# RWKV core of a hybrid decoder step: copies and products moved between the engines, a gate's scaling carried in factors, chain parts placed inside half rounds

## What is computed

```python
def _wkv_step(S, inp):
    r, k, v, w, kk, b = inp
    sa = jnp.einsum('bhij,bhj->bhi', S, -kk)
    S = S * w[:, :, None, :] + sa[..., None] * b[:, :, None, :] + v[..., None] * k[:, :, None, :]
    return S, jnp.einsum('bhij,bhj->bhi', S, r)

w_log = -jax.nn.softplus(-(w0 + jnp.tanh(mix(1) @ w1) @ w2)) - 0.5
decay = jnp.exp(-jnp.exp(w_log))
iclr = jax.nn.sigmoid(a0 + (mix(4) @ a1) @ a2)
kk = heads(k * k_k); kk = kk / jnp.maximum(jnp.linalg.norm(kk, axis=-1, keepdims=True), 1e-12)
k_h = heads(k * (1.0 + (iclr - 1.0) * k_a))
b_h = kk * heads(iclr)
S_T, o = lax.scan(_wkv_step, S0, xs)          # 512 tokens, 16 heads of 64
bonus = jnp.sum(r_h * k_h * r_k, axis=-1, keepdims=True) * v_h
```

## Time and profile before

| | us |
|---|---|
| median of 3 runs | 3632.11 |
| lowest, highest | 3629.02, 3633.79 |
| the profiled execution, time | 3627.32 |
| its span | 3625.5 |
| granted TensorE clock, mean | 0.983 |
| TensorE busy | 3442.5 (95%) |
| VectorE busy | 1941.2 (54%) |
| ScalarE busy | 1395.1 (38%) |
| GpSimd busy | 418.8 (12%) |

### The profile page before, as it was taken

How to read it: one execution, slowest core, us unless ns; L and a number is a source line. 1 busy time by engine, 2 the same in 40 slices (tenths; PEclk the granted TensorE clock), 3 DMA queues, 4 the chain that set the end, 5 groups by cost and what they waited for, 6 DMA issues and landing times.

```text
span 3625.5 us, 95343 instructions
## 1 busy us (share of the span) xinstructions
PE 3442.5 (95%) x40925; PEld 3228.3 (89%) x40925; DVE 1941.2 (54%) x3021; ACT 1395.1 (38%) x2344; POOL 418.8 (12%) x570
## 2 busy tenths in 40 slices
PE   7988899999999989999999999999899788999999
PEld 6977679999999855699999999999899666799999
DVE  7557755555346644365543446553374776465532
ACT  4535533443222533344432224442244454244421
POOL 0022221111000000011100101110000222211100
PEclk9999989999999999999999999999999999999999
DMA  3210002222222387422222222222222000122222
GB/s 121 93 38 5 4 26 93 81 85 85 87 87 80 121 305 297 171 84 81 81 90 88 88 82 84 81 86 88 88 76 88 10 4 27 40 85 86 81 90 85
DMA packets 97093, 314.74 MB, mean 87 GB/s; under 512 B 19074, under 2 KB 20354, under 8 KB 96018
## 3 DMA queue, kind: packets, MB, share of 16 engines
q1 hardware_dynamic: 88706, 288.79, 23.7%
q10 hardware_dynamic: 8080, 21.34, 1.6%
HBM read 297.30 MB, written 12.79 MB: 86 GB/s over the span
## 4 chain that ended last, share of the span: by engine, by line
PE 88%; DVE 7%; ACT 3%; issue 2%; DMA 0%; SPq 0%; DVEq 0%; ACTq 0%
PE ps L418 24%; PE ps L416 23%; PE ps L417 23%; PE ps L1462 4%; PE ps L1017 1%; PE ps L2045 1%; DVE m L1507 1%; PE ps L2144 1%; PE ps L1646 1%; PE ps L2080 1%; PE ps L1128 1%; PE ps L2100 1%; PE ps L1138 1%; DVE arb L1495 1%; PE ps L2052 1%
## 5 line engine op out<-in xcount | busy, mean ns | idle before, releaser
L416 PE MATMUL ps<-xh,wh 128*128 128x288 f32 x4656 | 1386.0, 298 | 3.0 <-DVE xl L2430 1.9
L418 PE MATMUL ps<-xh,wl 128*128 128x288 f32 x4656 | 1381.5, 297 | 0.0
L417 PE MATMUL ps<-xl,wh 128*128 128x288 f32 x4656 | 1358.7, 292 | 0.0
L391 ACT ACTIVATE wh<-raw 128x1024 fp32r<-128x1024 f32 x415 | 440.2, 1061 | 1247.5 <-PE ps L418 1209.4
L417 PEld LDWEIGHTS ps<-xl,wh 128*128 128x128 f32 x4656 | 888.9, 191 | 1.7 <-issue 0.5
L416 PEld LDWEIGHTS ps<-xh,wh 128*128 128x128 f32 x4656 | 876.1, 188 | 7.5 <-issue 3.5
L418 PEld LDWEIGHTS ps<-xh,wl 128*128 128x128 f32 x4656 | 873.6, 188 | 0.0
L398 DVE TENSOR_TENSOR wl<-raw,wh 128x1024 fp32r<-128x1024 f32 x415 | 508.4, 1225 | 519.7 <-ACT wh L391 513.8
L418 PE MATMUL ps<-hh,wl 128*128 128x288 f32 x1536 | 457.7, 298 | 0.0
L416 PE MATMUL ps<-hh,wh 128*128 128x288 f32 x1536 | 453.9, 295 | 0.0
L417 PE MATMUL ps<-hl,wh 128*128 128x288 f32 x1536 | 453.9, 295 | 0.0
(11 more groups left out here) (360 smaller groups left out, 4927.1 us busy)
## 6 DMA issues: line engine op xcount, KB each, us to landing
raw<-in_w SPq DMA_DIRECT2D x415, 512.0 KB, 3.5
kp<-in_cache_k SPq DMA_DIRECT2D x64, 512.0 KB, 5.5
vp<-in_cache_v SPq DMA_DIRECT2D x64, 512.0 KB, 5.8
rkv<-in_wkv ACTq DMA_DIRECT2D x2, 2048.0 KB, 9.7
out_wkvs<-rkv ACTq DMA_DIRECT2D x2, 2048.0 KB, 7.2
out_k<-qk ACTq DMA_DIRECT2D x1, 2304.0 KB, 8.2
out_v<-vg ACTq DMA_DIRECT2D x1, 2304.0 KB, 14.0
out_x<-x SPq DMA_DIRECT2D x8, 288.0 KB, 3.4
```

Source lines behind the costliest of these rows:

```text
L391: act.activation(wh[:, c % SPL], raw[:, c % RAWS], ACT.Copy).then_inc(s_hi, 1)
L416: pe.matmul(out, w_h, rhs_h, start=(first and k == 0), stop=False)
L417: pe.matmul(out, w_h, rhs_l, start=False, stop=False)
L418: mm = pe.matmul(out, w_l, rhs_h, start=False, stop=(last and k == nk - 1))
```

## The change

- d2 and d4 of the prompt's inverse become "move": VectorE copies them (one 128 x 256 copy). "cross" (d2t, d4t) goes to ScalarE, two half-height copies. Counts of a_e and a_d, and GpSimd's wait for d2t, follow.
- L1182 goes to ScalarE as an Identity with scale and bias 0.5, in piece 4 behind the second tanh; the scan waits for it.
- L1189 is dropped. zz1 stays a tanh, so t3 and kh carry a factor of 2 and b a factor of 2, pinv is taken with a bias of ln 0.5, and the bonus gets a factor 0.5.
- b's product moves from GpSimd to VectorE, (zz1 + 1) x kraw, in piece 10 behind the bonus product.
- In a stop TensorE's products are cut in two halves (2 chunks each): even place, first half, odd place, second half. On ScalarE, VectorE and GpSimd the whole of `inv_step` comes behind the odd place.

```diff
@@ -5,6 +5,8 @@
+import math
@@ -141,6 +143,7 @@
         qg8, gneps, eps, warm, root5 = small[:, 0:1], small[:, 1:2], small[:, 2:3], small[:, 3:4], small[:, 8:13]
+        halves, lnhalf = small[:, 4:5], small[:, 5:6]
         big = m.at
@@ -1178,17 +1181,13 @@
             if k == 4:
-                dve.wait_ge(a_zz, B.cnt(2, 1))
-                dve.tensor_scalar(zz0, zz0, 0.5, 0.5, ALU.mult, ALU.add).then_inc(a_sg, 1)
                 after(dve, a_ex, B.cnt(3, 0))
-                dve.wait_ge(a_sg, B.cnt(2, 1))
+                dve.wait_ge(a_sg, B.cnt(1, 1))
                 dve.tensor_tensor_scan(flat(csum[:, 0]), mview("scan", 0 if B.prompt else 1), flat(zz0), 0.0,
...
                 dve.wait_ge(a_zz, B.cnt(2, 2))
-                dve.tensor_scalar(zz1, zz1, 0.5, 0.5, ALU.mult, ALU.add).then_inc(a_sg, 1)
                 dve.wait_ge(a_cm, B.cnt(1, 1))
-                dve.wait_ge(a_sg, B.cnt(2, 2))
                 if B.prompt:
@@ -1209,7 +1208,7 @@
                 dve.wait_ge(a_kh, B.cnt(2, 1))
-                dve.scalar_tensor_tensor(kh[:, 0], t3, 1.0, row, ALU.add, ALU.mult).then_inc(a_kh, 1)
+                dve.scalar_tensor_tensor(kh[:, 0], t3, 2.0, row, ALU.add, ALU.mult).then_inc(a_kh, 1)
             if k == 10:
@@ -1220,9 +1219,11 @@
                     dve.tensor_tensor(t3, t3, B.per(PC["rk", j]), ALU.mult).then_inc(a_rk, 1)
+                dve.wait_ge(a_kk, B.cnt(1, 1))
+                dve.scalar_tensor_tensor(bb, zz1, 1.0, kraw[:, 0], ALU.add, ALU.mult).then_inc(a_bb, 1)
             if k == 13:
                 dve.wait_ge(a_bo, B.cnt(1, 1))
-                dve.tensor_tensor(B.row(rkv, KD), z, B.row(rkv, 2 * KD), ALU.mult).then_inc(a_bon, 1)
+                dve.scalar_tensor_tensor(B.row(rkv, KD), z, 0.5, B.row(rkv, 2 * KD), ALU.mult, ALU.mult).then_inc(a_bon, 1)
                 after(dve, a_co, B.tile(NCK, -2 * NCK))
@@ -1281,10 +1282,12 @@
                 half_tanh(act, B, zz1, KD).then_inc(a_zz, 1)
+                act.wait_ge(a_zz, B.cnt(2, 1))
+                act.activation(zz0, zz0, ACT.Identity, scale=0.5, bias=halves).then_inc(a_sg, 1)
             if k == 8:
...
                 act.wait_ge(a_cs, B.cnt(1, 1))
-                act.activation(pinv[:, 0], csum[:, 0], ACT.Exp, scale=DECAY).then_inc(a_ex, 1)
+                act.activation(pinv[:, 0], csum[:, 0], ACT.Exp, scale=DECAY, bias=lnhalf).then_inc(a_ex, 1)
                 act.wait_ge(a_cm, B.cnt(1, 1))
@@ -1303,9 +1306,6 @@
                 pool.tensor_tensor(pprev[:, 0], csum[:, 0], zz0, ALU.subtract).then_inc(a_cm, 1)
-            if k == 10:
-                after(pool, a_kk, B.cnt(1, 1))
-                pool.tensor_tensor(bb, kraw[:, 0], zz1, ALU.mult).then_inc(a_bb, 1)
             if k == 12:
@@ -1317,9 +1317,9 @@
             ktok=("kst", "ist", 0, "copy", "", "ktok", ()),
-            d2=("m2", "m1", 0, "copy", "", "m3", ("lt", "ktok")),
+            d2=("m2", "m1", 0, "move", "", "m3", ("lt", "ktok")),
             d2t=("m1", "m2", 2, "cross", "", "m4", ("et",)),
-            d4=("m4", "m3", 2, "copy", "", "m1", ("d2", "d2t")),
+            d4=("m4", "m3", 2, "move", "", "m1", ("d2", "d2t")),
             d4t=("m3", "m4", 0, "cross", "", "m2", ()),
@@ -1370,14 +1370,14 @@
             return [(name, part) for r in rounds_of(prompt) for part in range(2) for name in r
-                    if steps_of(prompt)[name][3] == "copy"]
+                    if steps_of(prompt)[name][3] in ("copy", "cross")]
...
                 for part in range(2):
-                    out += [(name, part) for name in r if steps_of(prompt)[name][3] != "copy"]
+                    out += [(name, part) for name in r if steps_of(prompt)[name][3] not in ("copy", "cross")]
                     if "lt" in r and prompt:
@@ -1433,9 +1433,9 @@
-        def inv_pe(pe, B, k, part):
+        def inv_pe(pe, B, k, part, behind):
             inv, names = steps_of(B.prompt), rounds_of(B.prompt)[k]
-            for name in names:
+            for name in names if not behind else ():
                 if name == "lt":
@@ -1453,7 +1453,7 @@
                         after(pe, a_d, B.own("d", others_of(B.prompt).index((need, part)) + 1))
-            for p in range(4 * part, 4 * part + 4):
+            for p in range(4 * part + 2 * behind, 4 * part + 2 * behind + 2):
                 for name in names:
@@ -1464,23 +1464,32 @@
                     mm = l_pe(pe, Bat(B.j, B.c + 1), p)
-            mm.then_inc(a_m, 1)
+            if behind:
+                mm.then_inc(a_m, 1)
...
-        def inv_act(act, B, k, part):
+        def inv_act(act, B, k, part, behind):
+            if not behind:
+                return
             sl, inv, of = slots[B.s], steps_of(B.prompt), slice(4 * part, 4 * part + 4)
...
                 _, _, bk, how, _, to, _ = inv[name]
-                if how == "copy":
-                    if name == "d4":
-                        act.wait_ge(a_p1, B.own("p", 1))
-                    act.wait_ge(a_m, B.own("m", 2 * k + part + 1))
-                    act.activation(sl[to][:, of], half_of(bk, part), ACT.Copy).then_inc(a_e, 1)
...
-        def inv_dve(dve, B, k, part):
+                if how not in ("copy", "cross"):
+                    continue
+                act.wait_ge(a_m, B.own("m", 2 * k + part + 1))
+                if how == "cross":
+                    for r, cross in zip(HEADS, HEADS[::-1]):
+                        op = act.activation(sl[to][r, of], half_of(bk, part)[cross], ACT.Copy)
+                else:
+                    op = act.activation(sl[to][:, of], half_of(bk, part), ACT.Copy)
+                op.then_inc(a_e, 1)
...
+        def inv_dve(dve, B, k, part, behind):
+            if not behind:
+                return
             sl, inv, names = slots[B.s], steps_of(B.prompt), rounds_of(B.prompt)[k]
@@ -1499,13 +1508,13 @@
                 _, _, bk, how, by, to, _ = inv[name]
-                if how == "copy":
+                if how in ("copy", "cross"):
                     continue
+                if name == "d4":
+                    dve.wait_ge(a_p1, B.own("p", 1))
                 dve.wait_ge(a_m, B.own("m", 2 * k + part + 1))
-                if how == "cross":
-                    for r, cross in zip(HEADS, HEADS[::-1]):
-                        op = dve.tensor_copy(sl[to][r, of], half_of(bk, part)[cross])
-                    op.then_inc(a_d, 1)
+                if how == "move":
+                    dve.tensor_copy(sl[to][:, of], half_of(bk, part)).then_inc(a_d, 1)
                 elif how == "add":
@@ -1517,14 +1526,16 @@
-        def inv_pool(pool, B, k, part):
+        def inv_pool(pool, B, k, part, behind):
+            if not behind:
+                return
             sl = slots[B.s]
...
             if k == 1 and part == 1 and B.prompt:
-                after(pool, a_d, B.own("d", others_of(True).index(("d2t", 1)) + 1))
+                after(pool, a_e, B.own("e", copies_of(True).index(("d2t", 1)) + 1))
                 pool.tensor_tensor(plus[:], sl["m4"][:], mview("ist").unsqueeze(1).to_broadcast([P, NCK, CT]),
@@ -1599,11 +1610,10 @@
                     for behind in range(2):
-                        if behind:
-                            inv_step(eng, inv, k, part)
                         for q, pos in enumerate(CHAIN_AT if chain else ()):
...
                                 chain_part(eng, chain, q // 3, q % 3)
+                        inv_step(eng, inv, k, part, behind)
                     for piece, pos in enumerate(PREP_AT if prep else LAST_AT):
@@ -2535,6 +2545,8 @@
             dve.memset(gneps[:], GN_EPS)
+            dve.memset(halves, 0.5)
+            dve.memset(lnhalf, math.log(0.5))
             dve.memset(eps[:], RMS_EPS)
...
```

## The result

The changed kernel takes 3656.9 us (median of four executions, 3650.4 to 3667.8) against 3631.5 us, a ratio of 1.0073 [1.0047, 1.0099]. It is slower by 25 us, outside the range of 3612 to 3645. So the two traces lie 40 us apart, the medians 25; lengths read from this trace are rather too long. Of the executions behind the experiments three are far off (one of the kernel before 9044 us, one of e7 3956, one of e8 4779); the ratios and the slope further down leave them out.

What follows compares the result with a forecast made beforehand. No engine is full, so only TensorE's waits at its 22 stops count. Twelve full halves -1.2, two first -0.7, two preparing +0.4, two of the sample group -0.6: -2 us of 3625.5; median taken as 3630, range 3612 to 3645.

Steps and rivals of the forecast that it cites:

- rivals A and C: A: same time, waits at stops 4, 14 and L1138 go but return at stop 7, chance 0.43; C: see rival C.
- the two halves that prepare the sample group: Tanh in eight pieces, scan 2 us later, but two products freed of the standstill: +0.4 us for both.
- Part 1, the scan's path: Stops 2 to 7: scan 1.0 us later behind ScalarE's copies and Identity; loss 0.7 us, between 0.2 and 1.3.
- The shift at stop 8: TensorE reaches stop 8 at about 355.85 instead of 355.2 us: 0.7 later, between 0.2 and 1.3.
- rival C: Slower: ScalarE's queue shifts stop 8 beyond the 0.9 us that later waits can swallow; at 1.5, 3642 us; chance 0.23.
- Part 2, b's product: Stops 9 to 13: without GpSimd's product VectorE doesn't stand still, both products take 1.36 against 1.57 us; gain 0.36, twice.
- Part 3, the split: Chain parts inside half rounds: 0.33 + 0.24 = 0.6 us gained at places 29-30, up to 0.3 lost at even-to-odd places.
- The gain of 0.6 us around place 30: Places 29-30: eviction goes first (0.66 in place of 0.99 us), and the part lies half a stop earlier (0.24).
- from there to the end VectorE's adds and masks set the pace, and those don't change: From stop 16, reached at -0.1 us, to the half's end: VectorE's unchanged work sets the pace.
- its sign, a wait of over 1.5 us at stops 6 and 7: Rival C's mark: TensorE's wait around stops 6 and 7 over 1.5 us.

Runs made afterwards that it cites:

- e7: Changed kernel with d2, d4 back on ScalarE and d2t, d4t on VectorE, zz0's scaling staying on ScalarE: 3631.73 us, 0.9995.
- e8: e3 with one wait more, GpSimd's addition of the identity to m1 waiting for r's factor on VectorE: 3619.93 us, 0.9960.
- e6: Changed kernel with zz0's scaling back on VectorE, d2t and d4t staying on ScalarE: 3635.86 us, 1.0010.
- e14: Changed kernel with whole rounds in stops 0 to 8 and the split in stops 9 to 21: 3642.96 us, 1.0028.
- e5: Changed kernel with unread filler products on TensorE, 4 and 6 pairs before two waits of the chain: 3646.35 us, 1.0033.
- e4: Changed kernel without the split (whole rounds, order inside a stop as before); copies, scaling and b's product as changed: 3639.66 us, 1.0027.
- e11: Changed kernel with the Identity moved ahead of the second tanh on ScalarE: 3660.05 us, 1.0080.
- e3: Kernel before with b's product on VectorE behind the bonus product, iclr's gate factor carried and L1189 dropped: 3619.77 us, 0.9965.
- e2: Changed kernel with copies and zz0's scaling taken back; b's product on VectorE, factors and split kept: 3625.58 us, 0.9982.
- e15: e3 with the split only in stops 9 to 15: 3619.94 us, 0.9961.
- e9: e4 with zz0's scaling back on VectorE, so moved copies and b's product in whole rounds: 3626.93 us, 0.9989.

## Why the prediction was wrong

**The missing step: TensorE's clock.** The sum took every wait of TensorE as so many microseconds, one for one. Nowhere does it ask what a wider gap does to the granted clock, though the earlier trace rows has the column, and shows 0.97 for the cores and 1.00 for the half. In the sum this is a term put at nothing. The runs price it in three ways. Within e6: 2.7 us a half between halves with and without the fall, with the state no later. Between the changed kernel and e14, at the same lateness of the state: 1.9 us by the spread, 2.1 over the half. Between the changed kernel and e5: 10.5 to 24 us. A fourth, weaker one is the spread of the executions themselves: over the 83 executions of the kernel before that went with the experiments, time falls by 1.7 us for each 0.001 of mean clock; the changed kernel has 0.974 against 0.981, 12 us by that slope. Ten full halves at 2.1 to 2.7 us make 21 to 27 of the 33 us that the cores lost in the profiled execution, the slowest of the four; over the medians, 25 us apart, it is 10.5 to 24 (e5), and nearer to the 12 of the slope if the other executions, with their higher clock, fell less often. In e5, where the clock is held, 3646.4 less up to 13.7 for the filler is 3633 or more: at a held clock the change would be between no difference and 13 us of loss. That is where rivals A and C stood. A second term was far off too: the two halves that prepare the sample group, put at +0.4 us, took some 7.5 more in the profiled execution. Their clock fell further as well; how much of it is the clock's was not tested.

**Part 1, the scan's path.** The walk through ScalarE's queue was right in order and in size: half-height copies 0.77 us a pair (0.8 taken), Identity 0.71 (0.62 taken), scan 1.1 us later (1.0 taken). The shift at stop 8 was put at 0.7, at most 1.3. With the clock held in most or all full halves it is 0.8 (e14), 1.1 (e5, filler included) and 1.2 us (e4), so inside the bounds but in their upper half, and in two of the three above the 0.9 from which the prediction let rival C decide. With the clock's fall it is 2.7. The term was sized for the scan; e11 shows that what counts is the state: 1.4 us late in the changed kernel (8.86 to 10.29). The prediction named sst behind the Identity, and put its lateness into the same 0.7.

**Part 2, b's product.** The mechanism is right, the size probably too small. The bonus product takes 0.75 us wherever GpSimd has no product beside it, 1.57 where it has. The Trainium skill (SBUF — State Buffer, "SBUF: two separate sides") says that a VectorE operation with two SBUF inputs and a GpSimd operation that reads SBUF exclude each other; e3 and e8 agree, with 1.57 to 0.75 and 0.97 to 0.69 us. I counted 0.36 us for each first half and 0.2 for a full one, some 3 us. By e3 it is 1.3 and 0.45, some 7 us, and 12.7 between the medians. The two profiled executions lie 5.8 us apart, so the traces have nothing more to place. e3's mean clock is 0.983 against 0.982 in the kernel before, so a part of it may be the clock's.

**Part 3, the split.** The gain of 0.6 us around place 30 is there: from the bonus sum to sst 5 3.99 us before, 3.40 after; 4.07 in e4, 4.03 in e3, 3.40 in e2. The step that failed is "from there to the end VectorE's adds and masks set the pace, and those don't change": I let the 0.6 stand in the sum all the same. If VectorE sets the pace there, chain parts that come earlier wait longer; that it is VectorE was not tested. From sst 5 to the end it is 6.69 us before and 7.33 after, 6.55 in e3 and 7.18 in e15, which has whole rounds there again. And what the split costs in the early stops, where it stands between ScalarE's copies and the chain's evictions, was not in the sum: with the queue it is 17 us (e4 to the changed kernel), nearly all by way of the clock, for where the clock is held the split kernel's half is as long as e4's (31.83): 32.3 in e5, of which up to 0.7 are the filler. With the scaling back on VectorE it is 8 to 9 (e9 to e6), and the four fallen halves of e6 make up the difference between the full halves (4 x 2.7 us against 10 x 1.04).

**The rivals.** C named the right place and the right engine. Its condition, over 0.9 us at stop 8, held in e5 and e4 and just not in e14; its sign, a wait of over 1.5 us at stops 6 and 7, is 1.37 us in the half shown and at most 1.8. It gave 3642, about what the kernel takes with the clock held in most halves (e14 3643, e4 3640), but the 14 us beyond that go with falls of the clock, which C doesn't have either. It was given 0.23 because the average of ScalarE, 16.2 of 32 us, left room; the table of 2 us windows would have shown in the kernel before that TensorE's thinnest stretch (busy 1.28 of 2.00 us, at 352 to 354) is just where the change adds waiting. That was to be had before the run. Whether the clock would then fall was not: e4 and e14 are thinner there and mostly keep it.

**What stays open.** Why the split brings the clock down where e4 and e14, with TensorE as thin, mostly keep it. Why e2 lies 6 us above e3 although its full halves are shorter. How the 25 us divide exactly between waiting and clock, since a filler that holds the clock costs time itself; a version with the same waits and the clock held for nothing was not found.

## What to carry to other kernels

When a change lets TensorE wait longer in a stretch where it is already thin, read its busy time and its granted clock there in windows of a few microseconds, and put the fall of the clock down as a term of its own, with a chance, since the busy time alone did not tell here whether it falls: where it fell it cost 2 to 2.7 us a half, on top of 1.4 us of lateness. Of work moved to an engine with room on average, count what then stands in front of the evictions that a serial chain on TensorE waits for, and not only the step that was moved. A gain in the middle of the half is no gain of the half until the rest has been followed to its end.

## What the runs showed of the hardware

The granted clock of TensorE fell inside a kernel whose TensorE is 95% busy, once in each of ten full halves, in the half shown after a stretch of 2 us in which it was busy 0.63 us, with no single wait above 1.4. From 326 to 332 us it stood at 1.2 GHz, while TensorE had no idle time at all. The same code did it in some halves and not in others, with the same busy time ahead (e6), and 0.53 busy in 2 us left it at 2.4 GHz in most halves of e4 and e14.

A half-height copy on ScalarE, 64 x 256, took 0.38 us, as long as the full-height one of 128 x 256, and a pair 0.77: a cross copy in two pieces costs twice the whole one. The Identity over 128 x 512 with scale and a bias column took 0.71 us; the Exp with the bias column also took 0.71, and the Exp without one 0.62.

Adding 10 pairs of unread 64 x 64 products at two places of a half made one kernel 10.5 us faster, whose clock had fallen in all ten full halves, and another 13.7 us slower, whose clock had fallen in one.
